# Small gaps between the on-chip buffers of a one-core fp32 kernel: the start addresses of x, y, z and the weights are moved apart

## The reference

```
for l in range(DEPTH):                      # DEPTH = 2
    h = x @ w_in[l]                         # 512x1024 @ 1024x6048
    y_hg  = _hgrn2_group(...)               # gated recurrence
    y_mla = _mla_group(...)                 # latent attention
    y_mem = _memory_group(...)              # attention into mem
    y = concatenate([y_hg * silu(g1), y_mla * silu(g2), y_mem * silu(g3)], -1)
    x = _layernorm(ALPHA * x + y @ w_out[l], ln_g[l], ln_b[l])
```

```
h = h + 0.5 * rms_norm(swiglu(rms_norm(h, g), w_gate, w_up, w_down), g2)
h = h + rms_norm(hybrid_mixer(rms_norm(h, g), ...), g2)
h = h + 0.5 * rms_norm(swiglu(...), g2)
h = h + rms_norm((p @ ple_w_proj) * sigmoid(rms_norm(h, g) @ ple_w_gate), g2)
```

## Time and profile before

| | us |
|---|---|
| median of three runs | 2092.77 |
| the profiled execution | 2095.08 |
| span of the profile, first to last instruction | 2093.2 |
| TensorE busy (matmuls) | 2066.5 |
| TensorE's weight loads, beside the matmuls | 1720.9 |
| VectorE, ScalarE, GpSimd busy | 1055.7, 818.8, 949.7 |
| mean granted TensorE clock | 0.998 |

### The profile page before, as it was taken

The page is one execution under the profiler, slowest core; times in us unless marked ns, Lnnn a source line. Parts: engine busy times, 40 slices in busy tenths (PEclk is TensorE's granted clock), DMA queues, the critical chain, the costliest instruction groups (busy, mean ns, idle before and its releaser), DMA issues.

```text
span 2093.2 us, 33796 instructions
## 1 busy us (share of the span) xinstructions
PE 2066.5 (99%) x13712; PEld 1720.9 (82%) x13712; DVE 1055.7 (50%) x1861; ACT 818.8 (39%) x1665; POOL 949.7 (45%) x734
## 2 busy tenths in 40 slices
PE   7999999999999999999999999999999999999998
PEld 7878888778978888778888888888888898888886
DVE  6273465535564375634564554443432537534574
ACT  5423325554424234555523232344523433233244
POOL 4543433232443533222457656643445337676533
PEclk9999999999999999999999999999999999999999
DMA  6422223122321212113133233333132223333322
GB/s 238 174 83 80 79 68 97 45 74 68 101 83 61 98 58 71 62 61 111 56 109 120 99 101 101 111 116 101 61 104 99 81 81 121 101 121 101 101 71 91
DMA packets 98684, 196.69 MB, mean 94 GB/s; under 512 B 3680, under 2 KB 12256, under 8 KB 98144
## 3 DMA queue, kind: packets, MB, share of 16 engines
q1 hardware_dynamic: 95072, 183.25, 26.7%
q10 hardware_dynamic: 3456, 11.27, 1.6%
HBM read 192.41 MB, written 2.10 MB: 93 GB/s over the span
## 4 chain that ended last, share of the span: by engine, by line
PE 57%; ACT 1%; DVE 1%; DMA 0%; issue 0%; DVEq 0%; ACTq 0%
PE ps L1048 15%; PE ps L1050 15%; PE ps L1049 15%; PE ps L1077 3%; PE ps L1076 3%; PE ps L1078 3%; PE ps L1189 1%; PE ps L1329 1%; PE ps L1197 0%; PE ps L1206 0%; PE ps L1352 0%; PE ps L1372 0%; PE ps L1361 0%; PE ps L1242 0%; PE ps L1224 0%
## 5 line engine op out<-in xcount | busy, mean ns | idle before, releaser
L998 POOL TENSOR_TENSOR wl<-raw,wh 128x512 fp32r<-128x512 f32 (+2 forms) x676 | 877.7, 1324 | 1038.2 <-ACT wh L1427 1028.2
L1427 ACT CAST wh<-raw 128x512 fp32r<-128x512 f32 (+2 forms) x692 | 378.5, 604 | 616.0 <-PE ps L1050 444.0
L1048 PE MATMUL ps<-xh,wh 128*128 128x512 f32 (+1 forms) x1376 | 514.1, 374 | 1.2 <-issue 1.2
L1050 PE MATMUL ps<-xh,wl 128*128 128x512 f32 (+1 forms) x1376 | 509.0, 370 | 0.0
L1049 PE MATMUL ps<-xl,wh 128*128 128x512 f32 (+1 forms) x1376 | 508.5, 370 | 0.0
L1048 PEld LDWEIGHTS ps<-xh,wh 128*128 128x128 f32 x1376 | 259.3, 188 | 46.1 <-issue 3.9
L1050 PEld LDWEIGHTS ps<-xh,wl 128*128 128x128 f32 x1376 | 259.1, 188 | 44.5
L1049 PEld LDWEIGHTS ps<-xl,wh 128*128 128x128 f32 x1376 | 259.3, 188 | 42.3
L1048 PE MATMUL ps<-wh,xh 128*128 128x512 f32 (+1 forms) x608 | 238.9, 393 | 0.2 <-issue 0.2
L1050 PE MATMUL ps<-wh,xl 128*128 128x512 f32 (+1 forms) x608 | 234.4, 386 | 0.0
L1049 PE MATMUL ps<-wl,xh 128*128 128x512 f32 (+1 forms) x608 | 234.4, 385 | 0.0
(11 more groups left out here) (304 smaller groups left out, 2985.0 us busy)
## 6 DMA issues: line engine op xcount, KB each, us to landing
raw<-w_in SPq DMA_DIRECT2D x58, 1024.0 KB, 5.2
raw<-w_out SPq DMA_DIRECT2D x20, 1024.0 KB, 5.2
raw<-f1g SPq DMA_DIRECT2D x10, 1024.0 KB, 5.1
raw<-f1u SPq DMA_DIRECT2D x10, 1024.0 KB, 5.0
raw<-f1d SPq DMA_DIRECT2D x10, 1024.0 KB, 5.0
raw<-f2g SPq DMA_DIRECT2D x10, 1024.0 KB, 5.1
raw<-f2u SPq DMA_DIRECT2D x10, 1024.0 KB, 5.2
raw<-f2d SPq DMA_DIRECT2D x10, 1024.0 KB, 5.0
```

The lines of the kernel that those rows point to most:

```text
L998: pool.tensor_tensor(wl[s], source(u, k), wh[s].bitcast(F32), ALU.subtract).then_inc(low_done, 1)
L1048: pe.matmul(o, still[0], move[0], start=k0 + k == 0, stop=False)
L1050: mm = pe.matmul(o, still[1], move[0], start=False, stop=k0 + k == b.ktiles - 1)
L1427: act.copy(wh[:, v % 3, k, 0:width], source(v, k)).then_inc(high_done, 1)
```

## The change

Three further buffers that nobody reads or writes are taken: `fill_weights` (64 bytes) between x and the weights, `fill_y` (128 bytes) between the weights and y, and `fill_back` (224 bytes) ahead of the work areas and z. No instruction is added, removed or moved on any engine; every line number behind L394 grows by 1 to 3. What changes is where the operands start:

| buffers | start before, modulo 512 | after, modulo 512 | before, modulo 64 | after, modulo 64 |
|---|---|---|---|---|
| xs, xh, xl | 32 | 32 | 32 | 32 |
| raw, wh, wl | 32 | 96 | 32 | 32 |
| yh, yl, side | 32 | 224 | 32 | 32 |
| few, work, work2, v_n, zh, zl | 448 | 352 | 0 | 32 |

The distance, modulo 512, from the start of the moving operand to the start of the stationary one that is loaded beside it follows from that:

| matmul | before | after |
|---|---|---|
| x streams, w is loaded | 0 | 64 |
| w streams, x is loaded | 0 | 448 |
| y streams, w is loaded | 0 | 384 |
| w streams, y is loaded | 0 | 128 |
| w streams, z (or few) is loaded | 416 | 256 |
| z streams, w is loaded | 96 | 256 |
| second half of the `by_columns` block (x streams, w is loaded) | 384 | 448 |

```
         sb("fill_front", [P, 28])
         xs = sb("xs", [P, T, D])
         xh, xl = sb("xh", [P, KD, SEQ], F32R), sb("xl", [P, KD, SEQ], F32R)
+        sb("fill_weights", [P, 16])
         raw = sb("raw", [P, 2, 4, 512])
         wh, wl = sb("wh", [P, 3, 4, 512], F32R), sb("wl", [P, 3, 4, 512], F32R)
+        sb("fill_y", [P, 32])
         yh, yl = sb("yh", [P, 4, SEQ], F32R), sb("yl", [P, 4, SEQ], F32R)
         side = sb("side", [P, 4096])
         cols = sb("cols", [P, NCOLS])
         level_mask = sb("level_mask", [P, LEVELS - 1, P // 4], U8)
+        sb("fill_back", [P, 56])
```

## The result

| | before | after |
|---|---|---|
| median (4 runs each, side by side) | 2094.09 us | 2114.64 us |
| fastest and slowest | 2092.75, 2095.67 | 2114.32, 2116.92 |
| ratio | | 1.0102 [1.009, 1.0114] |

The account below looks back on a forecast made before the run. It took TensorE's matmul pace, set by operand distance, as the bound; x, y and other engines' terms were 0 and z gained 5.1 us, so 2092.77 - 5.1 = 2087.7 us, range 2043 to 2139.

Parts of the forecast that it names:

- x and the weights, from 0 to 64 or 448: nothing: Matmuls pairing x and weights, 5184 of 512 or 416 columns and 768 of 256: new distances cost 0 us.
- y and the weights, from 0 to 128 or 384: nothing: Matmuls pairing y and weights, 1296 of 512 columns and 192 of 256: new distances cost 0 us.
- its own case: Whole kernel, multiples of 64 all cost what distance 0 costs: 2087.7 us, between 2085.5 and 2090.5; chance 0.42.
- The z term: Matmuls with z or few loaded (756) or z streaming (96), moved to distance 256: 5.1 us faster.
- The term for the other engines' operands: Other engines' operands, such as work, and transfers into it, at new addresses: -1 to +1 us, taken as 0.
- 428.8 ns: Plain float32 products of 512 columns: read as 3.43 us / 8 each, half column rate; changed by nothing.
- Rival 1: x and weights: distance 64 as bad as 96, period 128 or more; sum +31.6 us, 2124.4 us; chance 0.17.
- Rival 2: All pairs: every distance but 0 costs, y pays too, z wins nothing; +45.9 us, 2138.7 us; chance 0.17.
- Rival 3: All pairs: distance 0 is itself a collision that the gaps remove; 1993.5 us, or 2043 for half; chance 0.16.
- Rival 4: Whole kernel: addresses do nothing, z blocks are slow for another reason; 2092.8 us; chance 0.08.

Follow-up runs that it names:

- m1: Kernel of its own, TensorE alone, loaded operands at distances 0 to 496 from one stream; 512 columns: 226.7 ns at 0, 233.3 at 64.
- m2: Kernel of its own, TensorE alone, varying streamed widths, loaded columns and stream start; 512 columns, 128 loaded: 226.7 ns at distance 0, 233.3 at 64.
- e1: Kernel before with only the 64-byte gap between x and the weights; y and z keep their distances to the weights: 2116.03 us, ratio 1.0104.
- e2: Kernel before with only the 128-byte gap between the weights and y; x and z keep their distances: 2099.29 us, ratio 1.0028.
- e4: Kernel before with fill_front 64 bytes longer, so all starts move together and every distance stays: 2094.87 us, ratio 1.0004.
- e3: Kernel before with only a 96-byte gap ahead of the work areas and z, putting z at distance 0 from the weights: 2089.12 us, ratio 0.9978.
- e5: Kernel before with 256-byte gaps between x and the weights and between the weights and y, z at 256 from the weights: 2088.79 us, ratio 0.9974.
- m3: Kernel of its own, TensorE alone, groups of 36 varying preceding group and stream start; distance 16: 233.3 ns behind 64, 226.9 behind 0.
- e7: Kernel before with x at 32, the weights' high and low parts at 48, y and z at 64 modulo 512: 2115.69 us, ratio 1.011.

## Why the prediction was wrong

**The failed step is "x and the weights, from 0 to 64 or 448: nothing", and with it "y and the weights, from 0 to 128 or 384: nothing".** It took the period for 64 bytes. m1 shows 256: with 512 columns 64 costs 6.6 ns, 448 costs 2.1, 128 costs 6.6 (5.4 in m2, 4.5 in the kernel after). In the kernel, x's two directions and y came to +20.5 + 3.6 + 0.2 - 3.5 + 5.9 = +26.7 us, where the sum had 0; e1 and e2 confirm the two parts alone (+22.4 and +5.7). The prediction's range, 2043 to 2139 us, holds the measured 2114.6 only because it was drawn wide enough for the rivals; its own case, 2085.5 to 2090.5, does not.

**The reason the step failed is its evidence.** It rested on the earlier trace rows, 120.0 ns at distance 384 as at 0. The prediction called this weak because the runs are broken every 32 columns, and still let it decide. In the kernel after, the same block is at distances 64 (first half) and 448 (second half), and the second half takes 11.52 us for 96 again, as does the first where no wait breaks it (1392.59 to 1395.47, 2.88 us for 24):

```profile
1395.47 0.28 PE L1051 MATMUL ps<-xh,wh 128*128 128x256 f32 x1
...
1406.99 0.40 PE L1051 MATMUL ps<-xh,wh 128*128 128x512 f32 x1
```

That form shows 120.0 at 0, 64, 384 and 448, so it can't tell these distances apart. Its width was no help either: in m1 even an unbroken stream of 256 columns has 120.1 at 384, as good as the 120.0 at 0, while one of 512 columns loses 6.6 ns there. At distance 64 unbroken streams of 256 columns do react: in the trace of the kernel after, 120 of them take 13.70 us, 114.2 ns, against 120.6 before.

```profile
549.16 0.37 PE L1051 MATMUL ps<-xh,wh 128*128 128x256 f32 x1
...
562.86 0.39 PE L1051 MATMUL ps<-xh,wh 128*128 128x512 f32 x1
```

**What held.** The matmuls' pace bounds the kernel, and among starts at multiples of 32 bytes the distance between streamed and loaded operand sets it, not a common shift of them (e4). The z term was right: -5.1 forecast, -5.2 by paces, and -4.5 and -5.3 measured in e3 (z at distance 0) and e5 (z at 256). Here it had luck: it took every multiple of 64 for a good distance, and z went to 256, which is one by m1's period too. The term for the other engines' operands, 0 within 1 us, fits: e3 and e5 put `work` at 32 modulo 64 as the change does, and z's paces alone give their times within about 1 us. One reading was wrong without touching the sum: the 8 instructions behind 428.8 ns are 4 matmuls of 512 columns (L1382 stands in a loop of four), so a plain float32 matmul takes two of them.

**Rival 1** (64 as bad as 96) had the mechanism for x streaming and was mis-sized. Its price put 6.6 ns on all 5184 matmuls of x; x loaded, at 448, cost 2.2 in the kernel. It added 2.5 us for 256 columns, where 3.5 were gained. It let y go free at 128. Taken together 31.6 became 20.6.

**Rival 2** (all but 0 costs) was right that both x and y pay (8.6 us for y, where paces give 5.9), and wrong on z: at 256 z is as fast as at 0. Its reading of the earlier trace rows as counter-evidence to itself was unfounded.

**Rival 3** fell for 512 columns: no distance, place or number of loaded columns in m1 and m2 goes under the 226.7 ns of distance 0. Where the 13.4 ns over the column rate come from stays open. With 256 columns the rival was right in kind: half of the excess of 13.3 ns goes at distance 64 (120.0 to 113.3), and x won it.

**Rival 4** falls: the same fp32r instructions take 226.7 or 233.3 ns by the loaded operand's address alone (m1). With it falls, for the fp32r pairs, what the prediction drew from the rule of the Trainium skill (page "TensorE: Matmul & The Clock Gate", section "Step-by-step: what each phase is for") that loading the next weights takes no read bandwidth from the running matmul: that no distance matters. The plain float32 and bf16 pairs of m1 and m3 agree with it.

**What stays open.** Why the good distances for 512 columns are those near 0 modulo 256, why 16 has two states, why 128 differs between m1, m2 and the kernel, and why a start at 16 modulo 32 costs. The runs give the pattern and not its cause.

## What to carry to other kernels

Where TensorE runs dense fp32r matmuls of 512 columns and 128 loaded ones, keep the buffers that it streams and those that it loads beside them at equal starts modulo 256 bytes, and all starts at multiples of 32; bringing z, the last buffer that stood off, into line was worth 0.2 to 0.3% here, and a gap of 64 bytes between x and the weights cost 1%. For other widths measure first: with 256 columns distance 64 was the best. Before one group of rows is taken as evidence for a rule, ask whether that form of instruction reacts to the variable at all. And when most of a kernel's time hangs on a value that no trace shows, the short kernel that measures it alone is the first experiment to make.

## What the runs showed of the hardware that was not expected

- fp32r, 512 columns, 128 loaded: 226.7 to 234.3 ns by distance, with a period of 256 bytes (m1).
- The cheapest distance depends on the width: 64 is worst or nearly so for 512 columns (233.3) and best for 256 (113.3 against 120.0 at 0); 384 columns have 173.3 at 0, 173.4 at 64 and 175.8 at 128 (m2). It depends on the number of loaded columns too: with 64 loaded, 96 is the best (226.7 against 230.0 at 0, m2).
- A pace can depend on what ran before: distance 16 holds 226.7 or 233.3 over a whole group of 36 (m3), and 227.1 or 234.3 over stretches of 192 and 96 in a whole kernel (e7). Distance 128 has 233.3 in m1 and 232.1 in m2, cause open.
- Streams that start at 16 modulo 32 take 3 to 10 ns more than 226.7 at distances 0, 16, 256 and 496 (m3).
- bf16 and plain float32 pairs show none of it at the four distances tried: 215.8 for 512 columns of bf16, and 215.8 to 215.9 for each of the two instructions of a plain float32 matmul of 256.
